# A dilated attention of 8 heads rebuilt: token-major values, two heads a step, strips of 32 queries against 256 near keys

## What is computed

```python
for g, (window, dilation) in enumerate(DILATED_GROUPS):    # (128, 1), (512, 4), (2048, 16)
    q = apply_rotary(qkv[:, :, g, 0], cos, sin)
    k = apply_rotary(qkv[:, :, g, 1], cos, sin)
    o, lse = dilated_window_attention(q, k, qkv[:, :, g, 2], window, dilation)
    outs.append(o)
    lses.append(lse)
wts = jax.nn.softmax(jnp.stack(lses, axis=0), axis=0)
o = jnp.sum(wts[..., None] * jnp.stack(outs, axis=0), axis=0).astype(x.dtype)
```

## Time and profile before

| what | us |
|---|---|
| median of 3 runs | 3128.99 |
| the 3 runs | 3128.46, 3128.99, 3131.74 |
| the profiled execution | 3133.31 |
| its span on the core | 3131.5 |
| PE busy | 2953.7 |
| DVE busy | 1485.7 |
| ACT busy | 966.2 |
| mean granted TensorE clock | 0.961 |
| HBM read | 262.22 MB |

### The profile page before, as it was taken

How to read it: one execution, slowest core, us unless ns; L and a number is a source line. 1 busy time by engine, 2 the same in 40 slices (tenths; PEclk the granted TensorE clock), 3 DMA queues, 4 the chain that set the end, 5 groups by cost and what they waited for, 6 DMA issues and landing times. The chain is left out here.

```text
span 3131.5 us, 34488 instructions
## 1 busy us (share of the span) xinstructions
PE 2953.7 (94%) x12785; PEld 2343.0 (75%) x12800; DVE 1485.7 (47%) x1907; ACT 966.2 (31%) x1287; POOL 198.7 (6%) x209
## 2 busy tenths in 40 slices
PE   6999998879999999999989999999999998699997
PEld 5777876547888888887667888877767676488885
DVE  6575246365444344433755443248943234533323
ACT  4432223143332233322353332222223342322312
POOL 3000032001000000000300000000000000100000
PEclk9999998689999999999999999999988999899998
DMA  3334254122333233322202333234300023123321
GB/s 134 101 125 156 92 143 128 28 81 94 95 99 108 73 101 94 107 96 87 97 21 95 100 94 113 99 121 134 118 15 1 7 82 114 47 94 97 107 95 43
DMA packets 82403, 284.57 MB, mean 91 GB/s; under 512 B 14712, under 2 KB 15352, under 8 KB 81424
## 3 DMA queue, kind: packets, MB, share of 16 engines
q1 hardware_dynamic: 71392, 250.57, 25.0%
q0 software_dynamic: 6320, 26.63, 2.6%
q10 hardware_dynamic: 4608, 6.30, 0.7%
HBM read 262.22 MB, written 14.94 MB: 89 GB/s over the span
## 5 line engine op out<-in xcount | busy, mean ns | idle before, releaser
L178 DVE TENSOR_TENSOR wl<-raw,wh 128x1024 fp32r<-128x1024 f32 (+2 forms) x440 | 575.2, 1308 | 1050.5 <-ACT wh L172 1039.7
L222 PE MATMUL PS<-Hh,wl 128*128 128x512 f32 x2328 | 916.0, 393 | 41.6 <-DVE wl L178 18.8
L224 PE MATMUL PS<-Hl,wh 128*128 128x512 f32 x2328 | 908.8, 390 | 0.0
L223 PE MATMUL PS<-Hh,wh 128*128 128x512 f32 x2328 | 908.6, 390 | 0.0
L172 ACT ACTIVATE wh<-raw 128x1024 fp32r<-128x1024 f32 (+2 forms) x440 | 480.7, 1093 | 1103.4 <-PE PS L224 977.5
L222 PEld LDWEIGHTS PS<-Hh,wl 128*128 128x128 f32 x2328 | 438.9, 189 | 151.7 <-issue 40.8
L223 PEld LDWEIGHTS PS<-Hh,wh 128*128 128x128 f32 x2328 | 438.9, 189 | 91.2 <-issue 1.5
L224 PEld LDWEIGHTS PS<-Hl,wh 128*128 128x128 f32 x2328 | 438.4, 188 | 91.6
L224 PE MATMUL PS<-ffn_gl,wh 128*128 128x512 f32 x880 | 350.6, 398 | 0.0
L222 PE MATMUL PS<-ffn_gh,wl 128*128 128x512 f32 x880 | 346.1, 393 | 2.9 <-DVE wl L178 2.9
L223 PE MATMUL PS<-ffn_gh,wh 128*128 128x512 f32 x880 | 348.2, 396 | 0.0
(11 more groups left out here) (410 smaller groups left out, 2771.8 us busy)
## 6 DMA issues: line engine op xcount, KB each, us to landing
raw<-in_gu SPq DMA_DIRECT2D x220, 512.0 KB, 3.5
raw<-in_dn SPq DMA_DIRECT2D x80, 704.0 KB, 4.0
raw<-in_hin SPq DMA_DIRECT2D x44, 512.0 KB, 3.8
raw<-in_oin SPq DMA_DIRECT2D x16, 512.0 KB, 3.6
raw<-in_hin_gate SPq DMA_DIRECT2D x16, 512.0 KB, 3.5
X<-QKV ACTq DMA_DIRECT2D x96, 64.0 KB, 2.9
kept_x<-X POOLq DMA_DIRECT2D x16, 256.0 KB, 3.8
raw<-in_eout SPq DMA_DIRECT2D x8, 512.0 KB, 3.6
```

What stands on the lines that cost most here:

```text
L178: self.nc.vector.tensor_sub(self.wl[j % SPLIT][:, 0:kw], self.raw[j][:, 0:kw], self.wh[j % SPLIT][:, 0:kw].bitcast(F32)).then_inc(self.lo_ ...
L222: self.nc.tensor.matmul(out, wl, xh[:, u.k0 + k, :], start=first, stop=False)
L223: self.nc.tensor.matmul(out, wh, xh[:, u.k0 + k, :], start=False, stop=False)
L224: done = self.nc.tensor.matmul(out, wh, xl[:, u.k0 + k, :], start=False, stop=last)
```

## The change

The stages `turn_values` and `attend` go, and `window_attend` comes in their place. The three value turns of `hin` become token-major: their weights are laid out by `token_major`, they use banks 4 to 7, 0 to 3 and 4 to 7 in turn, and ACT reads four banks behind the last unit of each turn. PE's loop in `hybrid_input` is unrolled (it gets a `between` that does nothing). The stationary operand of the turns 9 and 10 is every fourth token.

`window_attend` has 16 steps of two heads and one residue. The near scores of the 128 queries are taken in four strips of 32 queries, each against the 256 keys around it, and each on its own 32 output partitions; so a row has 512 scores in place of 768. Masks are fp32 and DVE adds them (`mask` gives the view for a residue). A product with the diagonal of reciprocals divides and turns. Turned near probabilities of four residues are kept (`PTA`), and near values are weighed once per head pair, over 128 columns (4 residues x 32 queries) of a strip. `PTA` and `PTB` reuse memory that is free by then (`X`, query and key slots, `RS`, `SS`). The new function:

```diff
+def window_attend(co, QKV, MASK, PTA, PTB, OH, OL, scale):
     nc = co.nc
+    steps = [(c, r) for c in range(4) for r in range(4)]
+    n = len(steps)
+    with ExitStack() as ctx:
+        SC = co.sb("wa_sc", [P, 3, 2, S], ctx=ctx)
+        ST = co.sb("wa_st", [P, 3, 4, 2], ctx=ctx)
+        DG = co.sb("wa_dg", [P, 3, 2, P], ctx=ctx)
+        scored, masked, negated, powered, inverted, normed, turned, copied, weighted, out_hi, out_lo = (
+            co.sem(f"wa_{s}") for s in ("scored", "masked", "negated", "powered", "inverted", "normed", "turned", "copied",
+                                        "weighted", "out_hi", "out_lo"))
+        block = ctx.enter_context(nc.Block())
+        back = lambda t, c: t[:, c, :].rearrange("p (q r) -> p r q", r=4)
+        out_of = lambda c: co.PS[:, 6 + c % 2, :].rearrange("p (r q) -> p r q", r=4)
         @block.tensor
         def _(pe):
+            mm = nc.tensor.matmul
+            def scores(k):
+                c, r = steps[k]
+                if k >= 2:
+                    pe.wait_ge(masked, 2 * (k - 2) + 2)
+                for j in range(TT):
+                    first = P * max(j - 1, 0)
+                    for s in range(2):
+                        p = HD * s
+                        mm(co.PS[32 * j:32 * j + 32, 2 * (k % 2) + s, 0:2 * P],
+                           QKV[p:p + HD, c, j * P + r:(j + 1) * P:4], QKV[p:p + HD, 4 + c, first:first + 2 * P],
+                           start=True, stop=True)
+                for g in (1, 2):
+                    for s in range(2):
+                        p = HD * s
+                        m = mm(co.PS[:, 2 * (k % 2) + s, (1 + g) * P:(2 + g) * P], QKV[p:p + HD, 8 * g + c, r::4],
+                               QKV[p:p + HD, 8 * g + 4 + c, r::4], start=True, stop=True)
+                        if g == 2:
+                            m.then_inc(scored, 1)
+            def turn(k):
+                for s in range(2):
+                    pe.wait_ge(normed, 2 * k + s + 1)
+                    if k >= 1:
+                        pe.wait_ge(copied, 4 * (k - 1) + 2 * s + 2)
+                    for b in range(4):
+                        m = mm(co.PS[:, 4 + s, b * P:(b + 1) * P], SC[:, k % 3, s, b * P:(b + 1) * P],
+                               DG[:, k % 3, s, :], start=True, stop=True)
+                    m.then_inc(turned, 1)
+            def weigh(k):
+                c, r = steps[k]
+                pe.wait_ge(copied, 4 * k + 4)
+                if r == 0 and c >= 2:
+                    pe.wait_ge(out_lo, c - 1)
+                for g in (1, 2):
+                    for s in range(2):
+                        h = 2 * c + s
+                        m = mm(co.PS[HD * s:HD * s + HD, 6 + c % 2, r * P:(r + 1) * P],
+                               QKV[:, 24 + 4 * g + r, h * HD:(h + 1) * HD], PTB[k % 2][:, s, (g - 1) * P:g * P],
+                               start=g == 1 and r == 0, stop=False)
+                if r == 3:
+                    for j in range(TT):
+                        for b in range(2 if j else 1):
+                            for s in range(2):
+                                h = 2 * c + s
+                                at = PTA[c % 2][:, 2 * s + b, :].rearrange("p (r q) -> p r q", r=4)
+                                m = mm(out_of(c)[HD * s:HD * s + HD, :, 32 * j:32 * j + 32],
+                                       QKV[:, 24 + max(j - 1, 0) + b, h * HD:(h + 1) * HD], at[:, :, 32 * j:32 * j + 32],
+                                       start=False, stop=j == TT - 1 and b == 1)
+                m.then_inc(weighted, 1)
             for k in range(n + 3):
                 if k < n:
+                    scores(k)
                 if 2 <= k < n + 2:
+                    turn(k - 2)
                 if k >= 3:
+                    weigh(k - 3)
         @block.scalar
         def _(act):
             for k in range(n + 3):
                 if k < n:
                     act.wait_ge(negated, k + 1)
+                    for s in range(2):
+                        nc.scalar.activation(SC[:, k % 3, s, :], SC[:, k % 3, s, :], ACT.Exp, scale=scale,
+                                             bias=ST[:, k % 3, 1, s:s + 1], accum_out=ST[:, k % 3, 2, s:s + 1]).then_inc(powered, 1)
                 if 2 <= k < n + 2:
+                    c, r = steps[k - 2]
                     if k >= 4:
                         act.wait_ge(weighted, k - 3)
+                    for s in range(2):
+                        act.wait_ge(turned, 2 * (k - 2) + s + 1)
+                        if r == 0 and c >= 2 and s == 0:
+                            act.wait_ge(weighted, 4 * (c - 1))
+                        nc.scalar.activation(PTA[c % 2][:, 2 * s:2 * s + 2, r * P:(r + 1) * P],
+                                             co.PS[:, 4 + s, 0:2 * P].rearrange("p (b q) -> p b q", b=2),
+                                             ACT.Copy).then_inc(copied, 1)
+                        nc.scalar.activation(PTB[k % 2][:, s, :], co.PS[:, 4 + s, 2 * P:4 * P], ACT.Copy).then_inc(copied, 1)
+                if k >= 3 and steps[k - 3][1] == 3:
+                    c = steps[k - 3][0]
                     act.wait_ge(weighted, k - 2)
+                    nc.scalar.activation(back(OH, c), out_of(c), ACT.Copy).then_inc(out_hi, 1)
+        @block.vector
+        def _(dve):
+            v = nc.vector
+            for k in range(n + 3):
+                if k < n:
+                    c, r = steps[k]
+                    if k >= 3:
+                        dve.wait_ge(turned, 2 * (k - 3) + 2)
+                    for s in range(2):
+                        dve.wait_ge(scored, 2 * k + s + 1)
+                        v.tensor_tensor_reduce(SC[:, k % 3, s, :].rearrange("p (a b) -> p a b", a=2),
+                                               co.PS[:, 2 * (k % 2) + s, :].rearrange("p (a b) -> p a b", a=2), mask(MASK, r),
+                                               op0=ALU.add, op1=ALU.max, scale=1.0, scalar=NEG,
+                                               accum_out=ST[:, k % 3, 0, s:s + 1]).then_inc(masked, 1)
+                    dve.wait_ge(masked, 2 * k + 2)
+                    v.tensor_scalar(ST[:, k % 3, 1, :], ST[:, k % 3, 0, :], -scale, None, ALU.mult).then_inc(negated, 1)
+                if 1 <= k < n + 1:
+                    b = (k - 1) % 3
+                    dve.wait_ge(powered, 2 * k)
+                    v.reciprocal(ST[:, b, 3, :], ST[:, b, 2, :]).then_inc(inverted, 1)
+                    dve.wait_ge(inverted, k)
+                    for s in range(2):
+                        v.tensor_scalar(DG[:, b, s, :], co.ident, ST[:, b, 3, s:s + 1], None, ALU.mult).then_inc(normed, 1)
+                if k >= 4 and steps[k - 4][1] == 3 or k == n + 2:
+                    c = steps[k - 4][0] if k < n + 2 else 3
+                    dve.wait_ge(out_hi, c + 1)
+                    v.tensor_sub(back(OL, c), out_of(c), back(OH, c).bitcast(F32)).then_inc(out_lo, 1)
```

The rest of the diff, cut to its core:

```diff
-WINDOW = S + 4
-MW = WINDOW + 2 * P
+WINDOW = 2 * P + 4
+MW = 2 * WINDOW
+def mask(MASK, r):
+    first, step = 3 - r, WINDOW - 3 + r
+    return MASK[:, first:first + 2 * step].rearrange("p (a b) -> p a b", a=2)[:, :, 0:2 * P]
...
-            co.multiply(pe, st, bank_free)
+            co.multiply(pe, st, bank_free, between=lambda n: None)
...
-                elif i >= first_v:
+                elif i >= first_v and c == RAW - 1:
                     co.wait_units(act, st, i, c)
-                    nc.scalar.activation(one(QKV, 24 + RAW * (i - first_v) + c), one(co.PS, c),
-                                         ACT.Copy).then_inc(bank_free, 1)
+                    for t in range(TT):
+                        nc.scalar.activation(QKV[:, 24 + RAW * (i - first_v) + t, :], co.PS[:, st.tokens[i][1] + t, :],
+                                             ACT.Copy).then_inc(bank_free, 1)
...
-            nc.vector.tensor_copy(IB[:], co.ident).then_inc(cast, 1)
...
+    every4 = lambda t: slice(t, None, 4)
+    st["hin"].tokens = {8: (lambda t: slice(t * P, (t + 1) * P), 4, 1), 9: (every4, 0, 1), 10: (every4, 4, 1)}
...
-            MK = co.sb("MK", [P, MW], BF16, inner)
-            IB = co.sb("IB", [P, P], BF16, inner)
+            MASK = co.sb("MASK", [P, MW], ctx=inner)
...
+            near = [co.X[:, 4:8, :], QKV[:, 0:16:4, :]]
+            far = [t[:].rearrange("p (s n) -> p s n", s=2) for t in (co.RS, co.SS)]
+            window_attend(co, QKV, MASK, near, far, OH, OL, HD ** -0.5)
...
-    a["hin"] = blocked(np.concatenate([piece(n) for n in (10, 9, 0, 1, 3, 4, 6, 7, 2, 5, 8)], 1))
+    a["hin"] = np.concatenate([blocked(np.concatenate([piece(n) for n in (10, 9, 0, 1, 3, 4, 6, 7)], 1))] +
+                              [token_major(piece(n)) for n in (2, 5, 8)])
```

More of the change, by code:

```diff
@@ L2042, in _ @@
         @block.tensor
         def _(pe):
[L2044 to L2057, removed]
@@ L2105, in _ @@
-                if k >= 3:
-                    x = items[k - 3]
```

(26 more changed lines are left out.)

89 lines of the change are left out of this document (3 added, 86 removed).

## The result

The changed kernel takes 3011.9 us (median of 4 runs, 3007.4 to 3014.7), the kernel before 3130.4 (median of 4): a ratio of 0.962, with a 95% interval from 0.9604 to 0.9637. The forecast was 3023, its range 3003 to 3053. The gain is 118 us and was put at 106. The profiled execution took 3014.7 us.

What follows compares the result with a forecast made beforehand. PE (TensorE) was taken to bound the attention stretch. Savings of 99.5 us (stage) + 8.5 (joint) - 2 (strides) = 106 off 3133.3 gave 3027, as a median 3023; range 3012 to 3036, eight in ten 3003 to 3053.

Steps and rivals of the forecast that it cites:

- The bound: In the dilated attention PE sets the time: busy 161.7 of 165 us, against 51.7 for DVE and 50.2 for ACT.
- Near scores: New attention, per step: eight matmuls of 256 columns overlap in pairs, 1.91 us; ends 1.06 and 6.0.
- The rival with fourfold overlap: New attention: four strips run at once, near scores 1.06 us a step, total 3009 us; chance 0.10.
- Far scores, turning, weighing: New attention on PE: per step 1.2 us far scores, 1.98 diagonal products, 0.58 far weighing; near weighing 1.54 per head pair.
- Other engines: New attention: DVE under 3 us a step and ACT 2.9 lie beside PE's 6.1; the waits' cover is 0.7 us.
- Clock: New attention: half speed over some 6.8 us at the start, costing 3.4 us, then granted clock 1.00; ends none and 9.
- The rival of a falling clock: New attention: the clock keeps falling and a loss of 11% stays, 11 us, total 3034; chance 0.17.
- The joint: Between input projections and attention: without the turning of values, 12.3 us becomes 3.8, saving 8.5.
- The strides: Value turns with stationary columns at stride 4: 192 loads, 70 ns longer each but mostly hidden, cost 2 us; ends 0 and 13.
- the slower rival: New attention: each score matmul runs isolated, steps 12.1 us, or 20.1 at half clock, giving a total of 3244; chance 0.03.
- ACT's burst: Input projections: four copies after a value turn leave the split 0.2 us late, twice, costing nothing; 3.6 us if slack were missing.
- The written-out loop: Input projections: unrolling PE's loop costs nothing, hidden behind PE's queue of work.

Runs made afterwards that it cites:

- experiment 9: The changed kernel with each near and each far score matmul issued twice a step: 3026.3 us in one run.
- experiment 6: The changed kernel with heads outside the strips, far groups and near-weighing key blocks in the issue order: one run, attention 82.2 us, strips 0.62 a step.
- experiment 4: The changed kernel with DVE dividing the probabilities and PE transposing them, in place of diagonal products: 2998.8 us, ratio 0.9576 to the kernel before.
- experiment 3: The kernel before with the new attention alone, values still feature-major and turned in their own stage, PE's loop kept: 3016.1 against 3133.3 us, ratio 0.9623.
- experiment 5: The kernel before with its six transposes an item replaced by products with the fp32 identity: 3159.7 against 3135.3 us, ratio 1.0077.
- experiment 8: The kernel before with queries and far keys read contiguously in place of every fourth token: 3096.3 us in one run, attention 161.3 us.
- experiment 1: The kernel before with only PE's loop in the input projections written out: 3140.1 against 3133.3 us, ratio 1.0016.
- experiment 7: The changed kernel with PE's turns 1 to 7 of the input projections as a loop again: 3008.5 us against 3140.3 for the kernel before, ratio 0.9587.

## Why the prediction was right, and where it was off

**The bound.** PE sets the stretch in both kernels: by the waits it stood still for 1.5 us of the new stage once it had begun. That step held.

**Near scores.** This term was mis-sized: 1.91 us a step by pairs, and the runs show 0.63. The premise was that the second half of a matmul must wait for the first on its tile, so that only neighbours overlap. The trace shows eight records starting together and the other eight behind them, and experiment 9 that all of it streams at once; experiment 6 rules out that it hangs on the order. 16 x 1.28 = 20.5 us of the miss. The rival with fourfold overlap (chance 0.10) had the right mechanism and stopped halfway, at 1.06. The Trainium skill (TensorE: Matmul & The Clock Gate, Part 3) has tiles start some 4 ns apart. Here eight start within 0.06 us, 7 or 8 ns apart, so the trace agrees that they overlap and has them a little further apart. The row of the odd layer should have been given less weight against it, as it held only two tiles.

**Far scores, turning, weighing.** 1.23, 1.98 and 0.59 against 1.2, 1.98 and 0.58: durations of the odd layer carried over unchanged. The near weighing was put at 1.54 and took 1.63. By the steps a near weighing adds 1.5 to one. So the sum on PE becomes 16 x 4.43 + 4 x 1.5 = 77, the tail and its waits 4, the clock's start 3: 84.

**Other engines.** Both were hidden until the tail, as said. The cover was thin, as said, and experiment 4 shows what comes next: with 1 us less on PE, ACT's copies are late by 0.4 at every second step.

**Clock.** Forecast half speed for 6.8 us, then full; measured some 10 us low, then 1.00. That length varies: in the profiles of experiments 3 and 6, with the same attention, it is some 6 and 3 us, and their attention is 1.4 and 1.7 us shorter. The rival of a falling clock did not come about. The prediction took the full clock from the odd layer's row, and beside it named the transposes, with which the drops would go. They are not the reason: with transposes back the clock stays at 1.00 from 2307 to 2360 (experiment 4), and without them it still falls (experiment 5). The Trainium skill (the same page, Part 4) has transposes not count as busy; in the one stretch of transposes alone, the 48 of the turning from 2289 to 2296, the clock was 1.00, but that is short, and a longer one was not tried. In the attention they did not decide. The strided reads of single heads did: without the stride the clock stayed at 1.00 (experiment 8). They are still in the new kernel, but in pairs of heads and for 1.2 of 4.4 us; which of the two keeps the clock up was not tested, so this part of the forecast came true without its cause being known.

**The joint** saved 12.3 - 3.4 = 8.9, forecast 8.5. **The strides** of turns 9 and 10 were priced right: 192 matmuls at 235 ns against 227, 1.6 us against 2. Their weight loads grew by more than the 70 ns assumed, from 188 to 310 (the two values lie side by side in this group, which holds contiguous turns too), and were all but hidden:

```profile
L197 PEld LDWEIGHTS PS<-wh,Hh x128: 187/248/311, 1541.0 to 2295.0; 128*128 128x128 f32 x128
L197 PE MATMUL PS<-wh,Hh x128: 389/394/402, 1541.2 to 2295.2; 128*128 128x512 f32 x128
```

The Trainium skill's page SBUF — State Buffer (SBUF cachelines) speaks of such a penalty. These runs agree and show it where nothing hides the access: experiment 8 took 0.13 us off the near product, of which only the stationary operand was strided, and 0.34 off a far one, with both. One term of the slower rival was wrong by this: it doubled the far products' time at half clock, and their time does not change (experiment 8). **ACT's burst** of copies cost nothing, as said.

**The written-out loop** was costed at nothing, "hidden behind PE's queue of work". That step failed: 3 us between the readings (experiments 1 and 7), about 5 by experiment 1's total, and it eats most of what token-major values give. By the waits it lies in the chain from a reading through the swap and rotation to the next split, which has little slack: ACT's wait for the rotation, 13.5 us in all before, doubled in experiment 1. What starts the delay is not shown.

**The sum.** Saved by the traces: 119.4 in the stage and 8.9 in the joint, less 1.6 for strides and 2.9 between the readings, 123.8. The two profiled executions differ by 118.6; of the rest 4.5 are the first query reading, which came at 2087.9 before and 2092.4 after. To judge by its spread that is variation from one execution to the next: it came at 2085.5 to 2094.2 us in the profiles with the loop and at 2083.5 to 2094.5 in those without. So the error on the saving (118 against 106, 12 us) is 20 us of strips, less 3 to 5 of loop and some 4 of variation. The total lies in the wide range (3003 to 3053) and at the lower edge of the narrow one (3012 to 3036). That it isn't further off is in part luck: the cost that was put at nothing made up for some of the strips' gain.

## What to carry to other kernels

Eight small matmuls on different row halves and different output partitions could be counted together here, as the streaming of one of them plus a fixed 0.2 us, rather than by pairs. A product that divides and turns in one was the wrong trade where PE sets the pace, at twice the time of a transpose; whether it gains where PE has time to spare was not tried. When an edit is made for one stage's sake, run its parts alone; here one part's gain was spent by a side effect of itself, and keeping the loop where it was possible took that side effect away.

## What the runs showed of the hardware

Eight fp32 matmuls of 256 columns on eight tiles took 0.63 us, and twice as many 1.06. A stationary and a moving operand read at stride 4 (16 bytes) made a single-head product of 128 columns take 0.76 us in place of 0.42, and the granted clock, 0.88 in that stage once it had begun, was 1.00 over 124 us when they were contiguous. That strided product took 0.76 us at either clock. A load of 128 stationary columns took 310 ns at stride 4 and 188 contiguous. Writing a PE loop out, with the same matmuls, cost 0.16% of the kernel's time (0.05 to 0.26%).
